# Two of the four additions of each post norm moved to GpSimd, and the output stored by quarters

## The chip, the cores and the metric

The kernel runs on one core of a Trainium2 chip. The metric is the device time of one execution in microseconds; the median of several executions stands for a kernel. All times below are in microseconds unless marked otherwise.

## The reference, cut to what matters

The program computes three layers on a sequence of 256 tokens with 2048 features, in fp32: a first hybrid layer with a feed-forward part, an attention layer (`ev`) and a pooling layer (`od`). The two last ones end alike. The result of their output product is normalised over the features, multiplied by a gate and added to the residual:

```python
def _rmsnorm(x, g):
    xf = x.astype(jnp.float32)
    y = xf * lax.rsqrt(jnp.mean(xf * xf, axis=-1, keepdims=True) + EPS)
    return (y * g.astype(jnp.float32)).astype(x.dtype)

# end of the attention layer, then of the pooling layer
x = x + gate * _rmsnorm(y @ w_out, post_g)
```

Between them stands the pooling layer's first step, `h = _rmsnorm(x, pre_g) * (1 + scale) + shift`, and a product of `h` with a weight matrix. After the pooling layer `x`, 256 x 2048, is the output.

## The kernel before

Activations lie with features on the 128 partitions and tokens along the free axis: the residual `res` and the outputs of a product, `pr`, are 16 tiles of 128x256. Weights stream from HBM in halves of 512 KB (`w_main`, issued by SyncE). ScalarE rounds each to `w_hi`, VectorE makes the rest `w_lo`, and TensorE multiplies in three passes (lines 565 to 567). A second stream, `w_side`, is issued by GpSimd (line 490) and summed by VectorE into the modulation vectors.

Each engine has one program, and its order is the order in which the Python writes it; semaphores alone tie the engines together. An engine that waits holds back everything written behind the wait.

In the product before a post norm, VectorE reads each output tile times the gate into `pr` (line 1577), ScalarE squares it (line 1076) and GpSimd adds the squares up (`add_square`, line 531). TensorE then sums over the partitions with a matrix of ones (line 592), and `mean_to_rstd` turns that into `rstd` (line 1470, a square root on ScalarE at line 1103, a reciprocal at line 1472).

`post_norm` (lines 1492 to 1505) follows on VectorE. The 16 tiles are taken as four groups of four, 128x1024 each. For every group there is a product, `sq2 = pr * rstd` (line 1499), and an addition, `res = res + sq2` (line 1504), interleaved as product 0, product 1, addition 0, product 2, addition 1, product 3, addition 2, addition 3. Each addition increments the semaphore `ev_res` or `final`. The trace calls `sq2` simply `sq`, as it leaves numbers out of names.

After `ev_post`, the middle gap: ScalarE squares the groups of `res` in the order 0 to 3 (`squares`, line 1098), TensorE adds them with the matrix of ones (`norm`, line 650; eight instructions in the trace for a group of four tiles), and the next norm's `rstd`, its scaling and the product `od_u` follow.

After `od_post`, the end: TensorE transposes the groups of `res` in the order 0 to 3 (line 644 through `turn`), ScalarE copies the half with the first 128 tokens to `o_tok` (line 1397), VectorE the half with the last 128 (line 2121). VectorE's copies are written behind all of its `post_norm`. SyncE stores `o_tok` in four DMAs of 512 KB (line 479): features 0 to 1023 of the first and of the last tokens, then 1024 to 2047 of both, each behind a wait for its copies.

Of the kernel before, what the change touches and what calls it, by code (L numbers as in the profile page):

```python
# [29 lines left out]
P = 128  # L30
# [158 lines left out]

SUMMED = ("ffn", "ev", "ev_post", "od_post")
NORMS = ("ffn", "ev", "od")
ROOTS = ("ffn", "ev", "ev_post", "od", "od_post")
# [49 lines left out]
def build(nc, x, ctx_in, w_main, w_side, cols_in, cons_in, gla_masks_in, counts_in, gate_w2_in, cmp_w2_in, out):  # L244
    stack = ExitStack()
    with stack:
# [182 lines left out]
        @block.sync  # L429
        def _(sp):  # L430
            sp.dma_start(cons[:, 0:2 * P], cons_in[:, 0:2 * P]).then_inc(S("ident_in"), 16)
            for q in range(4):
                part = slice(q * D // 4, (q + 1) * D // 4)
                sp.dma_start(x_tok[:, :, part], x.rearrange("(a p) d -> p a d", p=P)[:, :, part])\
                  .then_inc(S(f"x_in{q}"), 16)
                if q == 0:
                    sp.dma_start(cols[:, :], cols_in).then_inc(S("cols_in"), 16)
            for h in range(4):
                sp.dma_start(raw[:, h, :], w_main[stored_half(h // 2, h % 2)]).then_inc(raw_full[h], 16)
            sp.dma_start(cons[:, 2 * P:NCONS], cons_in[:, 2 * P:NCONS]).then_inc(S("small_in"), 16)  # L440
            sp.dma_start(table[:, 0:7 * P], gla_masks_in).then_inc(S("small_in"), 16)
            sp.dma_start(gate_w2[0:16, :], gate_w2_in).then_inc(S("small_in"), 16)
            sp.dma_start(cmp_w2[:, :, :], cmp_w2_in).then_inc(S("small_in"), 16)

            def load(i, h, at):

                sp.wait_ge(lo_ready, i * 4 + (h - 3))
                src = w_main[at] if isinstance(i, int) else w_main[bass.ds(i * 4 + at, 1)].rearrange("a p n -> (a p) n")
                sp.dma_start(raw[:, h % 4, :], src).then_inc(raw_full[h % 4], 16)

            def loads(stage):

                s0, s1 = max(FIRST[stage], 2), FIRST[stage] + COUNT[stage]
                stored = 2 * (STORED[stage] - FIRST[stage])

                def pair(i, s, count=2):
                    for h in range(2 * s, 2 * (s + count)):
                        load(i, h, h + stored)
                with sp.Fori(0, (s1 - s0) // 2) as i:
                    pair(i, s0)  # L460
                if (s1 - s0) % 2:
                    pair(0, s1 - 1, 1)

            for h in range(4, 2 * FIRST_LAYER):
                load(0, h, stored_half(h // 2, h % 2))
            for stage, count in STAGES:
                if FIRST[stage] < FIRST_LAYER:
                    continue
                loads(stage)
                if stage == "down0":  # L470

                    sp.wait_ge(dve_read, dve_reads("down0"))
                    sp.dma_start(ctx_tok[:, :, :], ctx_in.rearrange("(a p) d -> p a d", p=P)).then_inc(S("ctx_in"), 16)
                    sp.dma_start(table[:, :], counts_in).then_inc(S("counts_in"), 16)
            for part in range(2):
                cut = slice(part * D // 2, (part + 1) * D // 2)
                for tt in range(TT):
                    sp.wait_ge(S(f"o_tok{tt}"), 2 * part + 2)
                    sp.dma_start(out[tt * P:(tt + 1) * P, cut], o_tok[:, tt, cut]).then_inc(S("stored"), 16)
            sp.wait_ge(S("stored"), 16 * 2 * TT)  # L480


        @block.gpsimd
        def _(pool):
# [35 lines left out]
            def add_square(n, k):  # L520

                at0 = square_at(SUMMED[n])
                if k == 0:
# [7 lines left out]
                pool.tensor_tensor(sq_sum[:, :], sq_sum[:, :], sq_tile[:, k % 2, :], ALU.add)\  # L531
                    .then_inc(S("squares_added"), 1)

            def mods_and_squares(m0, n):

                for k in range(16):
                    add_square(n, k)
                    side_load(0, m0 + k + 2 * CMP_HALVES, (mods_added, m0 + k - 1))
# [8 lines left out]
                add_square(1, k)  # L547
            mod_loads(group_start("ev_kv") + 2, group_start("ev_out") + 2)
            mods_and_squares(group_start("ev_out") + 2, 2)
            mod_loads(group_start("od_z") + 2, 2 * MOD_TILES)  # L550
            for k in range(16):
                add_square(3, k)


        @block.tensor
        def _(pe):
# [87 lines left out]
                return pe.transpose(ps[0:ncols, bank, at_col:at_col + rows], src_ap, ident[base:base + rows, base:base + rows])  # L644

            def norm(name, bank=2):
                for q in range(4):
                    pe.wait_ge(S(f"{name}_sq"), q + 1)
                    for f in range(4 * q, 4 * q + 4):
                        mm = pe.matmul(ps[:, bank, 0:T], ones, sq[:, f, :], start=f == 0, stop=f == 15)  # L650
                mm.then_inc(S("sums_ready"), 1)
# [367 lines left out]
                    sum_mods("od_z")  # L1019
            pe.wait_ge(silu_ready, FFN_TILES + 33)  # L1020
            run("od_out", (b_hi, b_lo), split=[("gate_lo", FFN_TILES + 16)], summed="od_post")
            for g in range(4):
                pe.wait_ge(S("final"), g + 1)
                for tt in range(TT):
                    for f in range(4 * g, 4 * g + 4):
                        mm = turn(res[:, f, tt * P:(tt + 1) * P], 4 * tt + g, (f % 4) * P)
                    mm.then_inc(S("o_t"), 1)
# [26 lines left out]
        def _(act):  # L1054
# [38 lines left out]
                    square(0, COUNT[stage] - 1)  # L1093

            def squares(name, src, dst, wait):
                for q in range(4):
                    wait(q)
                    act.activation(dst[:, 4 * q:4 * q + 4, :], src[:, 4 * q:4 * q + 4, :], ACT.Square)\
                       .then_inc(S(f"{name}_sq"), 1)
# [263 lines left out]
            root("ev_post", rstd[:, :])  # L1363


            squares("od", res, sq, lambda q: act.wait_ge(S("ev_res"), q + 1))
            root("od", rstd[:, :])
            shift_hi("od", sq, a_hi, lambda f: mods[:, 48 + f, 0:1])
            def pool_chain():
# [22 lines left out]
                       .then_inc(S("od_hi"), 1)  # L1392
            ahead("od_out", squared="od_post")
            root("od_post", rstd[:, :])
            for g in range(4):
                act.wait_ge(S("o_t"), 2 * g + 1)
                act.activation(o_tok[:, 0, g * 512:(g + 1) * 512], ps[:, g, :], ACT.Copy).then_inc(S("o_tok0"), 1)


# [1 line left out]
        def _(dve):  # L1401
# [89 lines left out]
                                                       op0=ALU.add, op1=ALU.subtract)  # L1491
                    ins.then_inc(S("norm_lo"), 1)

            def post_norm(name, done):

                mean_to_rstd(name, ps[:, 2, 0:T], rstd[:, :], D)
                for q in range(5):
                    if q < 4:
                        dve.tensor_tensor(sq2[:, 4 * q:4 * q + 4, :], pr[:, 4 * q:4 * q + 4, :], cbc(rstd[:, :], 4), ALU.mult)\
                           .then_inc(S(f"{name}_y"), 1)  # L1500
                    if q > 0:
                        part = slice(4 * q - 4, 4 * q)
                        dve.wait_ge(S(f"{name}_y"), q)
                        dve.tensor_tensor(res[:, part, :], res[:, part, :], sq2[:, part, :], ALU.add)\
                           .then_inc(S(done), 1)

            link = S("dve_link")
            links = [0]
# [536 lines left out]

            reading("ev_z", z_read(0, 16, (a_hi, a_lo)), chain=chain)
            reading("ev_out", gated_read(ev_gate))
            post_norm("ev_post", "ev_res")
            dve.wait_ge(S("ev_res"), 4)


            dve.wait_ge(S("mods_read"), MOD_STAGES.index("ev_z") + 1)
# [62 lines left out]
            dve.wait_ge(S("mods_read"), len(MOD_STAGES))  # L2115
            then(dve.tensor_tensor(od_gate[:, :], mods[:, 80:96, 0], col("od_post", 0, 16), ALU.mult))
            reading("od_out", gated_read(od_gate))
            post_norm("od_post", "final")
            for g in range(4):
                dve.wait_ge(S("o_t"), 2 * g + 2)  # L2120
                dve.tensor_copy(o_tok[:, 1, g * 512:(g + 1) * 512], ps[:, 4 + g, :]).then_inc(S("o_tok1"), 1)


# [117 lines left out]
```

## Time and profile before

| | before |
|---|---|
| median of 3 executions | 2099.07 |
| lowest, highest | 2090.81, 2099.28 |
| the profiled execution | 2097.16 |
| its span | 2095.2 |
| TensorE busy | 2040.4 (97%) |
| VectorE busy | 1561.3 (75%) |
| ScalarE busy | 895.0 (43%) |
| GpSimd busy | 171.9 (8%) |
| TensorE's mean granted clock | 0.984 |

The span runs from the first to the last instruction of the profiled execution; the time of that execution is 1.96 longer. Busy times are sums over the span; they say little of the two gaps that the change touches, which last some ten microseconds each and are read from the timelines.

### The profile page before, as it was taken

Reading aid. Unit: us, or ns where it says so; the run is one execution under the profiler, and the core shown is the slowest. Engines: PE = TensorE matmul, PEld = TensorE weight load, DVE = VectorE, ACT = ScalarE, POOL = GpSimd, SP = SyncE. Lnnn points to the kernel's source line nnn. Section 1 sums busy time; section 2 is a strip of 40 time slices with the busy share of each in tenths; the row PEclk is TensorE's granted clock in tenths of the full one; section 3 lists DMA queues with packets and bytes.
Section 4 is the critical chain, followed back from the end, with each engine's and each line's share of the span. In section 5 each row is a group of like instructions: output and inputs, shape, how many; then the busy total and the mean of one; then the engine's idle time right before and its main releaser. Section 6 shows DMA issues by size and latency. Waiting matters only on the chain.

```text
span 2095.2 us, 41764 instructions
## 1 busy us (share of the span) xinstructions
PE 2040.4 (97%) x16266; PEld 1988.4 (95%) x16266; DVE 1561.3 (75%) x2056; ACT 895.0 (43%) x1178; POOL 171.9 (8%) x264
## 2 busy tenths in 40 slices
PE   7999999999999999999999998999999997999997
PEld 6999998899999999999999998998889996999996
DVE  6985576657777867787878888678887777677755
ACT  6553446554343334333333454235454444344442
POOL 0000000021000000000011111010000120000010
PEclk9999999999999999999999999999999998999998
DMA  6444453255666776666878864565556772558552
GB/s 229 161 162 136 167 184 119 101 178 205 230 228 224 261 277 222 228 224 236 272 259 295 299 224 172 172 247 197 199 171 224 262 274 105 192 204 277 195 187 98
DMA packets 119578, 434.46 MB, mean 207 GB/s; under 512 B 13216, under 2 KB 13600, under 8 KB 119216
## 3 DMA queue, kind: packets, MB, share of 16 engines
q1 hardware_dynamic: 90672, 328.11, 45.8%
q0 software_dynamic: 28800, 104.87, 14.2%
q8 instruction: 74, 1.21, 0.2%
q14 instruction: 32, 0.26, 0.0%
HBM read 430.83 MB, written 2.10 MB: 207 GB/s over the span
## 4 chain that ended last, share of the span: by engine, by line
PE 90%; DVE 7%; ACT 1%; issue 1%; DMA 1%; POOL 0%; SPq 0%; POOLq 0%; DVEq 0%; ACTq 0%
PE ps L565 27%; PE ps L567 26%; PE ps L566 26%; DVE w_lo L1407 2%; PE ps L644 1%; PE ps L968 1%; PE ps L639 1%; PE ps L978 1%; PE ps L683 1%; ACT w_hi L1062 0%; DVE pr L1563 0%; PE ps L674 0%; PE ps L919 0%; PE ps L650 0%; DVE rstd L1472 0%
## 5 line engine op out<-in xcount | busy, mean ns | idle before, releaser
L1062 ACT ACTIVATE w_hi<-raw 128x1024 fp32r<-128x1024 f32 x610 | 632.3, 1055 | 638.0 <-PE ps L567 625.5
L565 PE MATMUL ps<-a_hi,w_hi 128*128 128x256 f32 x3024 | 865.2, 286 | 6.3 <-DVE a_lo L1490 4.3
L566 PE MATMUL ps<-a_lo,w_hi 128*128 128x256 f32 x3024 | 858.3, 284 | 0.0
L567 PE MATMUL ps<-a_hi,w_lo 128*128 128x256 f32 x3024 | 858.1, 284 | 0.0
L1407 DVE TENSOR_TENSOR w_lo<-raw,w_hi 128x1024 fp32r<-128x1024 f32 x610 | 734.8, 1246 | 109.7 <-ACT w_hi L1062 108.6
L565 PEld LDWEIGHTS ps<-a_hi,w_hi 128*128 128x128 f32 x3024 | 583.2, 193 | 12.3 <-issue 7.5
L566 PEld LDWEIGHTS ps<-a_lo,w_hi 128*128 128x128 f32 x3024 | 583.4, 193 | 1.0 <-issue 1.0
L567 PEld LDWEIGHTS ps<-a_hi,w_lo 128*128 128x128 f32 x3024 | 583.0, 193 | 0.0
L565 PE MATMUL ps<-b_hi,w_hi 128*128 128x256 f32 x1920 | 553.6, 288 | 5.2 <-DVE b_lo L1490 4.6
L566 PE MATMUL ps<-b_lo,w_hi 128*128 128x256 f32 x1920 | 546.5, 285 | 0.0
L567 PE MATMUL ps<-b_hi,w_lo 128*128 128x256 f32 x1920 | 546.5, 285 | 0.0
L565 PEld LDWEIGHTS ps<-b_hi,w_hi 128*128 128x128 f32 x1920 | 371.7, 194 | 7.8 <-issue 7.2
L566 PEld LDWEIGHTS ps<-b_lo,w_hi 128*128 128x128 f32 x1920 | 371.9, 194 | 1.5 <-issue 1.4
L567 PEld LDWEIGHTS ps<-b_hi,w_lo 128*128 128x128 f32 x1920 | 371.8, 194 | 0.0
L1424 DVE SCALAR_TENSOR_TENSOR mod_sum<-side,csil,mod_sum 128x1024 f32<-128x1024 f32 x180 | 228.0, 1280 | 10.7 <-DMA side<-w_side 7.1
L490 POOL DMA_DIRECT2D side<-w_side x200 | 109.1, 546 | 1462.9 <-DVE mod_sum L1424 822.9
L1040 ACT ACTIVATE sg<-up_x 128x256 f32<-128x256 f32 x44 | 18.4, 417 | 232.5 <-DVE up_x L1934 232.5
L1424 DVE SCALAR_TENSOR_TENSOR mod_odd<-side,csil,mod_odd 128x1024 f32<-128x1024 f32 x60 | 74.2, 1278 | 0.6 <-DMA side<-w_side 0.6
L1934 DVE TENSOR_TENSOR up_x<-ps,rstd 128x256 f32<-128x256 f32 x88 | 37.0, 421 | 47.3 <-PE ps L567 47.2
L1582 DVE TENSOR_TENSOR pr<-ps,rstd 128x256 f32<-128x256 f32 x29 | 12.3, 423 | 69.7 <-PE ps L567 69.7
L531 POOL TENSOR_TENSOR sq_sum<-sq_sum,sq_tile 128x256 f32<-128x256 f32 x45 | 42.0, 933 | 192.8 <-ACT sq_tile L1076 192.8
L1841 DVE TENSOR_TENSOR res<-ps,res 128x256 f32 (+1 forms) x48 | 20.3, 423 | 33.4 <-PE ps L567 33.3
(308 smaller groups left out, 1291.2 us busy)
## 6 DMA issues: line engine op xcount, KB each, us to landing
raw<-w_main SPq DMA_DIRECT2D x610, 512.0 KB, 4.3
side<-w_side POOLq DMA_DIRECT2D x200, 512.0 KB, 4.5
x_tok<-x_in SPq DMA_DIRECT2D x4, 512.0 KB, 7.4
ctx_tok<-ctx_tok SPq DMA_DIRECT2D x1, 2048.0 KB, 11.4
y_out<-o_tok SPq DMA_DIRECT2D x4, 512.0 KB, 3.2
table<-counts_tab SPq DMA_DIRECT2D x1, 512.0 KB, 12.9
cons<-cons_in SPq DMA_DIRECT2D x1, 478.0 KB, 10.4
table<-masks_in SPq DMA_DIRECT2D x1, 448.0 KB, 10.3
```

Of the source, the lines that this page charges most:

```text
L490: pool.dma_start(side[:, n % 2, :], src).then_inc(side_full[n % 2], 16)
L531: pool.tensor_tensor(sq_sum[:, :], sq_sum[:, :], sq_tile[:, k % 2, :], ALU.add)\
L565: pe.matmul(out_ap, wh, act_hi[:, kt, :], start=first and n == 0, stop=False)
L566: pe.matmul(out_ap, wh, act_lo[:, kt, :], start=False, stop=False)
L567: mm = pe.matmul(out_ap, wl, act_hi[:, kt, :], start=False, stop=last and n == len(blocks) - 1)
L639: mm = pe.matmul(ps[:, MOD_BANK.get(stage, 7), vecs * t + c:vecs * t + c + 1], summed[c][:, t * P:(t + 1) * P], ones[:, 0:1], start=True, ...
L644: return pe.transpose(ps[0:ncols, bank, at_col:at_col + rows], src_ap, ident[base:base + rows, base:base + rows])
L683: mm = pe.matmul(ps[:, 7, 32 * kv:32 * kv + 2 * N_CMP], side[:, c % 2, b * P:(b + 1) * P], n_x[:, kv, j, :], start=j == 0, stop=j == CMP_W ...
L1062: act.activation(w_hi[:, slot, :], raw[:, slot, :], ACT.Copy).then_inc(hi_ready, 1)
L1407: dve.tensor_tensor(w_lo[:, slot, :], raw[:, slot, :], w_hi[:, slot, :].bitcast(F32), ALU.subtract)\
L1424: ins = dve.scalar_tensor_tensor(out=summed[c], in0=side[:, n % 2, :], scalar=value, in1=summed[c], op0=ALU.mult, op1=ALU.add)
L1934: dve.tensor_tensor(up_x[:, k % 2:k % 2 + 1, :], psum_tile(bank), rstd_row, ALU.mult)\
```

## The change

The constant `POST_ORDER = (0, 2, 1, 3)` is new. VectorE makes all four products, in the order 2, 0, 3, 1, and the additions of groups 0 and 1. GpSimd adds groups 2 and 3, each behind a wait for its product. ScalarE's squares, TensorE's sums, the transposes and the copies take the groups in the order 0, 2, 1, 3. The semaphores `post_added` and `post_pool` replace `ev_res` and `final`. The output goes out in eight DMAs of 256 KB, by groups of 512 features.

```diff
+POST_ORDER = (0, 2, 1, 3)
@@ sync
-            for part in range(2):
-                cut = slice(part * D // 2, (part + 1) * D // 2)
+            for n, g in enumerate(POST_ORDER):
+                part = slice(g * 512, (g + 1) * 512)
                 for tt in range(TT):
-                    sp.wait_ge(S(f"o_tok{tt}"), 2 * part + 2)
-                    sp.dma_start(out[tt * P:(tt + 1) * P, cut], o_tok[:, tt, cut]).then_inc(S("stored"), 16)
-            sp.wait_ge(S("stored"), 16 * 2 * TT)
+                    sp.wait_ge(S(f"o_tok{tt}"), n + 1)
+                    sp.dma_start(out[tt * P:(tt + 1) * P, part], o_tok[:, tt, part]).then_inc(S("stored"), 16)
+            sp.wait_ge(S("stored"), 16 * 4 * TT)
@@ gpsimd
+            def post_additions(name):
+
+                for q, made in ((2, 1), (3, 3)):
+                    part = slice(4 * q, 4 * q + 4)
+                    pool.wait_ge(S(f"{name}_y"), made)
+                    pool.tensor_tensor(res[:, part, :], res[:, part, :], sq2[:, part, :], ALU.add)\
+                        .then_inc(S("post_pool"), 1)
...
             mods_and_squares(group_start("ev_out") + 2, 2)
+            post_additions("ev_post")
             mod_loads(group_start("od_z") + 2, 2 * MOD_TILES)
             for k in range(16):
                 add_square(3, k)
+            post_additions("od_post")
@@ tensor
             def norm(name, bank=2):
-                for q in range(4):
-                    pe.wait_ge(S(f"{name}_sq"), q + 1)
+                for n, q in enumerate(POST_ORDER):
+                    pe.wait_ge(S(f"{name}_sq"), n + 1)
...
-            for g in range(4):
-                pe.wait_ge(S("final"), g + 1)
+            for g in POST_ORDER:
+                pe.wait_ge(S("post_added" if g < 2 else "post_pool"), g % 2 + 3)
@@ scalar
             def squares(name, src, dst, wait):
-                for q in range(4):
+                for q in POST_ORDER:
...
-            squares("od", res, sq, lambda q: act.wait_ge(S("ev_res"), q + 1))
+            squares("od", res, sq, lambda q: act.wait_ge(S("post_added" if q < 2 else "post_pool"), q % 2 + 1))
...
-            for g in range(4):
-                act.wait_ge(S("o_t"), 2 * g + 1)
+            for n, g in enumerate(POST_ORDER):
+                act.wait_ge(S("o_t"), 2 * n + 1)
@@ vector
-            def post_norm(name, done):
+            def post_norm(name):
 
                 mean_to_rstd(name, ps[:, 2, 0:T], rstd[:, :], D)
-                for q in range(5):
-                    if q < 4:
-                        dve.tensor_tensor(sq2[:, 4 * q:4 * q + 4, :], pr[:, 4 * q:4 * q + 4, :], cbc(rstd[:, :], 4), ALU.mult)\
-                           .then_inc(S(f"{name}_y"), 1)
-                    if q > 0:
-                        part = slice(4 * q - 4, 4 * q)
-                        dve.wait_ge(S(f"{name}_y"), q)
-                        dve.tensor_tensor(res[:, part, :], res[:, part, :], sq2[:, part, :], ALU.add)\
-                           .then_inc(S(done), 1)
+
+                def part(q):
+                    return slice(4 * q, 4 * q + 4)
+
+                def product(q):
+                    dve.tensor_tensor(sq2[:, part(q), :], pr[:, part(q), :], cbc(rstd[:, :], 4), ALU.mult)\
+                       .then_inc(S(f"{name}_y"), 1)
+
+                def addition(q, made):
+                    dve.wait_ge(S(f"{name}_y"), made)
+                    dve.tensor_tensor(res[:, part(q), :], res[:, part(q), :], sq2[:, part(q), :], ALU.add)\
+                       .then_inc(S("post_added"), 1)
+
+                product(2)
+                product(0)
+                addition(0, 2)
+                product(3)
+                product(1)
+                addition(1, 4)
...
-            post_norm("ev_post", "ev_res")
-            dve.wait_ge(S("ev_res"), 4)
+            post_norm("ev_post")
+            dve.wait_ge(S("post_added"), 2)
+            dve.wait_ge(S("post_pool"), 2)
...
-            post_norm("od_post", "final")
-            for g in range(4):
-                dve.wait_ge(S("o_t"), 2 * g + 2)
+            post_norm("od_post")
+            for n, g in enumerate(POST_ORDER):
+                dve.wait_ge(S("o_t"), 2 * n + 2)
```

## Rows read from the trace of the kernel before

**Rows 1.** The page, the chain that ended last: shares of the span by engine.
```profile
PE 90%; DVE 7%; ACT 1%; issue 1%; DMA 1%; POOL 0%; SPq 0%; POOLq 0%; DVEq 0%; ACTq 0%
```

**Rows 2.** The same chain, its end: start, duration, what.
```profile
2079.16 2.36 DVE sq L1499 x2
...
2086.06 2.27 DVE res L1504 x2
2088.33 1.80 DVE o_tok L2121 x3
```

**Rows 3.** Timeline of VectorE after `ev_out`: start, duration, instruction, idle time before.
```profile
1747.29 2.36 DVE L1499 TENSOR_TENSOR sq<-pr,rstd 128x1024 f32<-128x1024 f32 x2
1749.57 1.22 DVE L1504 TENSOR_TENSOR res<-res,sq 128x1024 f32<-128x1024 f32 x1
...
1754.11 2.35 DVE L1504 TENSOR_TENSOR res<-res,sq 128x1024 f32<-128x1024 f32 x2
```

**Rows 4.** Timeline of ScalarE after `ev_out`.
```profile
1750.82 1.06 ACT L1098 ACTIVATE sq<-res 128x1024 f32<-128x1024 f32 x1 [5.35 <-DVE res L1504]
```

**Rows 5.** Timeline of TensorE after `ev_out`.
```profile
1751.93 8.85 PE L650 MATMUL ps<-sq,cons 128*128 128x256 f32 x32 [7.37 <-ACT sq L1098]
```

**Rows 6.** Windows, line 650: length, TensorE busy, weight loads, granted clock, DMA share, GB/s.
```profile
1751.90:1755.30 3.40, 3.37 (x8) 2.74 (x9) 0.50 0.00 0
1755.40:1760.80 5.40, 5.38 (x25) 4.38 (x24) 1.00 0.01 3
```

**Rows 7.** Timeline of GpSimd, additions of 128x256 in three stretches.
```profile
1737.63 0.94 POOL L531 TENSOR_TENSOR sq_sum<-sq_sum,sq_tile 128x256 f32<-128x256 f32 x1 [4.29 <-ACT sq_tile L1076]
...
2035.02 0.95 POOL L531 TENSOR_TENSOR sq_sum<-sq_sum,sq_tile 128x256 f32<-128x256 f32 x1 [4.79 <-ACT sq_tile L1076]
...
2074.91 0.72 POOL L531 TENSOR_TENSOR sq_sum<-sq_sum,sq_tile 128x256 f32<-128x256 f32 x1 [5.02 <-ACT sq_tile L1076]
```

**Rows 8.** Timeline of GpSimd, additions of 128x512.
```profile
444.05 2.37 POOL L517 TENSOR_TENSOR f_sum<-f_sum,f_sq 128x512 f32<-128x512 f32 x1 [4.85 <-ACT f_sq L1267]
...
478.32 1.30 POOL L517 TENSOR_TENSOR f_sum<-f_sum,f_sq 128x512 f32<-128x512 f32 x1 [3.10 <-ACT f_sq L1267]
```

**Rows 9.** Groups of GpSimd by line, shapes apart: busy, mean ns, idle before.
```profile
L502 POOL MEMSET g_k<- 128x1024 f32 x1 | 1.0, 954 | 0.0
```

**Rows 10.** Timeline of VectorE beside the first of rows 8.
```profile
442.92 2.35 DVE L1407 TENSOR_TENSOR w_lo<-raw,w_hi 128x1024 fp32r<-128x1024 f32 x2
```

**Rows 11.** Timeline of VectorE beside the first two of rows 7.
```profile
1737.88 1.76 DVE L1407 TENSOR_TENSOR w_lo<-raw,w_hi 128x1024 fp32r<-128x1024 f32 x1
...
2034.16 2.89 DVE L1407 TENSOR_TENSOR w_lo<-raw,w_hi 128x1024 fp32r<-128x1024 f32 x2
```

**Rows 12.** Timeline of ScalarE, the last square of `od_out`.
```profile
2074.45 0.38 ACT L1076 ACTIVATE sq_tile<-ps 128x256 f32<-128x256 f32 x1 [5.37 <-DVE pr L1577]
```

**Rows 13.** Timeline of VectorE at the end.
```profile
2088.25 2.47 DVE L2121 COPY o_tok<-ps 128x512 f32<-128x512 f32 x4
```

**Rows 14.** Timeline of TensorE at the end.
```profile
2082.71 1.97 PE L644 MATMUL ps<-cons,res 128*128 128x128 f32 x8 [6.28 <-DVE res L1504]
...
2087.25 2.23 PE L644 MATMUL ps<-cons,res 128*128 128x128 f32 x16 [0.49 <-DVE res L1504]
```

**Rows 15.** Windows at the end: busy times by engine, granted clock, DMA share, GB/s.
```profile
2082.00:2087.00 5.00, 3.75 (x16) 3.11 (x16) 5.00 (x5) 1.20 (x2) 0.00 (x0) 0.56 0.00 0
2087.00:2090.00 3.00, 2.19 (x16) 1.72 (x16) 3.00 (x5) 1.19 (x2) 0.00 (x0) 1.00 0.43 175
...
2090.50:2091.50 1.00, 0.00 (x0) 0.00 (x0) 0.23 (x1) 0.00 (x0) 0.00 (x0) 1.00 1.00 401
```

**Rows 16.** Line 479, SyncE's issues of the stores: ns min/median/max, first and last start.
```profile
L479 SPq DMA_DIRECT2D y_out<-o_tok x4: 348/392/453, 2086.8 to 2090.8; - x4
DMA to landing us min/median/max: 2.6/3.2/4.1
```

## The prediction

> **What bounds the kernel now.** I read the page's chain of waits first: TensorE carries 90% of it and VectorE 7% [rows 1]. The kernel is a row of matrix stages that keep TensorE full, and everything this change edits lies in two of the gaps between them: after the product `ev_out` (post norm `ev_post`, then the next norm's squares and sums) and after `od_out` (post norm `od_post`, then transposes, copies and stores). Nothing in the matrix stages is touched, so the question is only how long these two gaps get.
>
> The chain's end shows the last gap: eight VectorE instructions from 2079.16 to 2088.33, then VectorE's copies, then the stores [rows 2]. VectorE is in sequence on it all the way. The earlier gap has the same eight from 1747.29 on; the first addition ends at 1749.57 + 1.22 = 1750.79 and the last at 1754.11 + 2.35 = 1756.46 [rows 3]. Here only the first addition sets the end: ScalarE squares its group at once, 1.06 [rows 4], TensorE starts its sums at 1751.93 and runs them for 8.85 without a gap [rows 5]. So the middle gap is bound by the first addition and then by TensorE, with eight instructions for each of the four groups. Eight of the 32 fall into the 3.40 with a granted clock of 0.50 (1.2 GHz), 25 (one of them reaches in from before) into the 5.40 with 1.00 (2.4 GHz) [rows 6]: a group takes 8 x 0.43 = 3.4 at the low level and 8 x 0.216 = 1.73 at the full one. The squares of the last two additions are ready before TensorE wants them.
>
> **What the change does, part by part.** VectorE issues six instead of eight: product 2, product 0, addition 0, product 3, product 1, addition 1. GpSimd does additions 2 and 3. VectorE's start-to-start distance is 1.14 (a pair of 2.36 less 1.22) [rows 3].
>
> *GpSimd's addition of 128x1024.* No row has it. Alone, 128x256 takes 0.72 [rows 7] and 128x512 takes 1.30 [rows 8], so 0.58 for each further 256 columns: 1.30 + 2 x 0.58 = 2.46, an estimate. Bounds: twice the 512 row, 2.60, and from below a GpSimd instruction of that width that only writes, 0.95 [rows 9]. I take 2.46, as the rows are of the same operation. The Trainium skill (GPSIMD Engine Reference, Performance versus the Vector engine) gives 4497 ns for an addition of 2048 elements, half of which is 2.25; by that every figure below with two GpSimd additions would be 0.4 lower.
>
> *Do the two engines run beside each other?* This decides the sign. The six VectorE instructions all have both inputs in SBUF, and so do GpSimd's. The trace has such pairs. At 444.05 a GpSimd addition takes 2.37 while VectorE makes `w_lo`; at 478.32, with VectorE nearly idle, the same takes 1.30 [rows 8]: 1.07 more, about one VectorE instruction, and that VectorE pair took its usual 2.35 [rows 10]. The other way round, VectorE's `w_lo` at 1737.88 took 1.76 where 1.22 is usual; GpSimd's addition ended at 1737.63 + 0.94 = 1738.57, and VectorE ended 1.07 after that [rows 7, 11]. At 2034.16 a back-to-back pair took 2.89 instead of 2.35, and GpSimd, which had asked at 2035.02 in the middle of the first, took 0.95 [rows 7, 11]: it got in at 2035.97 - 0.72 = 2035.25, before the second of the pair. So they exclude each other, and a waiting GpSimd is served at the next boundary between VectorE instructions. What no row has is a GpSimd instruction of four times that width holding VectorE. I take it that the whole 2.46 is held, since in both rows VectorE was kept until GpSimd's end and not for a share of it; the other bound is no hold at all. The Trainium skill (SBUF — State Buffer, practical consequences) says that a VectorE instruction with two SBUF inputs contends with a GpSimd instruction that reads SBUF, and that the one that starts first keeps the shared ports for the whole instruction. By that rule the whole 2.46 is held; by the rows alone only about 0.7 is proven.
>
> *The timetable,* from the start of the first product, with full exclusion. Product 2 ends at 1.22, product 0 at 2.36. GpSimd is woken at 1.30 (0.08 from ScalarE's end 2074.83 to GpSimd's 2074.91 [rows 7, 12]), waits for product 0 and gets in at 2.23 (0.13 before its recorded end, as at 2035.25). Addition 0 has to wait for product 0's end, so GpSimd is first: addition 2 runs to 4.69. Addition 0 ends 1.07 later, at 5.76, where before it ended at 3.50. Product 3 ends at 6.89 and product 1 at 8.03; addition 3 gets in at 7.90 and ends at 10.36; addition 1 ends at 11.43. Before, all was done at 9.17. The added waits themselves (a VectorE instruction on the one just before it, twice) cost at most 0.1 each and lie inside GpSimd's time here. Each addition that is moved takes 1.14 off VectorE and puts 2.46 between two VectorE instructions.
>
> *Middle gap.* Addition 0 ends at 1747.29 + 5.76 = 1753.05, its square at 1754.14, TensorE starts at 1754.25 instead of 1751.93. Group 0 at the low clock lasts to 1757.7, group 2 to 1759.4. Addition 1 ends at 1758.72, its square at 1759.8, and the square of group 3 at 1760.9. Group 1 runs from 1759.9 to 1761.6, group 3 to 1763.4. With the same tail of about 0.1 that is 1763.5, where it was 1751.93 + 8.85 = 1760.78: **+2.7**. All after it hangs on these sums (rstd, `a_hi`, `a_lo`, `od_u`) and moves with them. Behind GpSimd's new waits stand only the side loads of the next modulation groups, whose data VectorE adds from `od_u` on; hidden, and at 0.
>
> *End.* Addition 1 ends at 2079.16 + 11.43 = 2090.59 instead of 2088.33 for the last of before. VectorE's copies (2.47 for four, 0.60 apart [rows 13]) come behind it: groups 0 and 2 end at 2091.2 and 2091.8. Groups 1 and 3 need transposes: 16 take 2.23 at full clock, 8 take 1.97 at the low one [rows 14]; the clock was low at 2082 to 2087 and full after [rows 15]. The last copy ends between 2093.3 and 2094.9. The stores: eight of 256 KB instead of four of 512 KB, on SP in one queue. The first leaves early, the second has to wait for VectorE's first copy at 2091.2, and six more stand behind it, also ScalarE's, which were long ready. An issue takes 0.39 [rows 16]; seven of 0.42 apart put the last at 2093.8 or later. At 401 GB/s [rows 15] 256 KB take 0.65, and seven 4.6. Before, the last of the four was issued at 2090.8 and 4.1 is the longest time to landing [rows 16], so about 2094.9. Its 1.57 MB with the two ahead of it take 3.9 at that rate, so they began at 2090.6 at the latest, and I put the data 0.9 behind the first of their issues, an estimate (VectorE's second copy, for which it waits, ends 2089.6). Now: 2091.2 + 0.9 + 4.6 = 2096.7, landing noted 0.4 later, and the rest of the span 0.4: 2097.5 against 2095.2, **+2.3**. If quarters travelled worse than 512 KB pieces the term would be up to 1 higher; if they let the data start earlier, 0.5 lower.
>
> **Sum.** +2.7 + 2.3 = +5.0. The profiled execution took 2097.16 with a span of 2095.2, so 2102.2 on its own basis. The median of the three runs shown is 1.9 above it, 2099.07, which gives 2104.1. I name 2103.1, between the two. With 0.95 for GpSimd's addition the timetable would have addition 0 at 4.25 and addition 1 at 8.41: +0.8 and about -1.0, so -0.2 in all; with 2.60 it is +5.4.
>
> **Rivals.**
> - *The two engines run side by side after all* (the other side: not slower). Its place is both timetables, and the point from which it decides is a GpSimd addition that ends while VectorE's instructions keep 1.22. Addition 0 ends at 3.6, addition 2 at 3.8, addition 3 and addition 1 at 7.2 instead of 9.17. The middle gap gains nothing, since TensorE is its bound (+0.1). At the end copies finish at about 2089.0 and stores, still one after another, at 2093.2: -2.0. Together -1.9: 2097.2 from the median, 2095.3 from the profiled execution. For it: nothing but that no row has this width. Against it: [rows 7, 8, 11].
> - *VectorE wins the port at the boundary*, because addition 0 needs product 0's end and is quick to ask. Then addition 0 ends at 3.6, addition 2 at 5.9, addition 1 at 9.4 and addition 3 at 11.7. Middle +1.2, end +1.0: +2.2: 2101.3 from the median, 2099.4 from the profiled execution, 2100.3 between them. Against it: GpSimd was served within a back-to-back pair [rows 7, 11].
> - *TensorE's clock stays low in the middle gap,* since TensorE now idles 9.7 instead of 7.4 before the sums [rows 5], then has a short hole ahead of group 1. Groups at 3.4 each from 1754.25: 1768.0, so +7.3 there; with slower transposes (+1) and the rest, +10.6: 2108.7, on the same footing as the forecast. For it: the first 3.4 of before were at 1.2 GHz. Against it: the clock rose about 3.4 after TensorE began, with the same kind of work [rows 6].
>
> **Chances.** Full exclusion, GpSimd first: 0.64. Side by side 0.12, VectorE first 0.12, low clock 0.12. All lie within 0.5% (10.5) of 2099.07, which is about what a measurement of this kernel can tell from no change. The three runs shown spread from 2090.81 to 2099.28, more than any rival moves, so a median may come out low for that reason alone (2103.1 - 8 = 2095). The range: 2094.5 to 2108. Faster by over 0.5% needs under 2088.6: 0.02. Slower by over 0.5% needs over 2109.6, the low clock and some more: 0.05. Same 0.93.
>
> **What would show it.** GpSimd's first addition of each post norm is recorded with 3.3 to 3.5 (2.46 and a wait of 0.9), the second likewise; VectorE's additions with over 3 instead of 1.22. TensorE's sums of the middle gap start 2.3 later and have a hole before their third group. SP's last seven issues follow one another without gaps from the first VectorE copy. I am wrong if VectorE's additions stay at 1.22 while GpSimd is at work, if GpSimd's additions are recorded under 2, or if the time before the middle gap differs between the two traces by more than these gaps do.

## The result, and the profile after

| | before | after |
|---|---|---|
| median | 2097.24 (20 executions) | 2099.25 (20 executions) |
| lowest, highest | 2090.63, 2100.57 | 2096.79, 2106.4 |
| span of the profiled execution | 2095.2 | 2096.7 |
| reciprocal to reciprocal in the middle gap | 16.30 | 19.06 |
| last reciprocal to the end of the span | 17.77 | 20.64 |

The ratio of after to before is 1.0022, with a 95% interval from 1.0011 to 1.0032: the change costs some 4.6 (2.3 to 6.7). The means say the same (2095.86 and 2100.47), while the medians are only 2.0 apart. The prediction named +5.0 and 2103.1, within 0.5%; the median came out 3.9 lower. Each of the five `rstd` ends in one reciprocal on VectorE, so the last three serve as marks: the middle gap is read from the third to the fourth, the end from the fifth. (The tails here and below are counted to some 0.05 before the end of the span, in all kernels alike, so their differences hold.) The middle gap grew by 2.76 and the end by 2.87, 5.6 together. The span grew by 1.5 only, because the stages ahead of both gaps, where the two kernels are the same, were shorter by 4.0 in this execution; the last section comes back to that.

Timeline of GpSimd after the change, both gaps (start, duration, instruction, idle time before it):

```profile
1744.56 3.24 POOL L540 TENSOR_TENSOR res<-res,sq 128x1024 f32<-128x1024 f32 x1 [4.27 <-DVE sq L1513]
1750.10 3.26 POOL L540 TENSOR_TENSOR res<-res,sq 128x1024 f32<-128x1024 f32 x1 [2.29 <-DVE sq L1513]
...
2079.13 3.25 POOL L540 TENSOR_TENSOR res<-res,sq 128x1024 f32<-128x1024 f32 x1 [4.79 <-DVE sq L1513]
2084.68 3.26 POOL L540 TENSOR_TENSOR res<-res,sq 128x1024 f32<-128x1024 f32 x1 [2.29 <-DVE sq L1513]
```

Timeline of VectorE in the middle gap, the answer to [rows 3]:

```profile
1741.45 1.75 DVE L1483 RECIPROCAL rstd<-rstd 128x256 f32<-128x256 f32 x1 [0.48 <-ACT rstd L1114]
1743.24 2.36 DVE L1513 TENSOR_TENSOR sq<-pr,rstd 128x1024 f32<-128x1024 f32 x2
1745.64 3.25 DVE L1518 TENSOR_TENSOR res<-res,sq 128x1024 f32<-128x1024 f32 x1
1748.81 2.35 DVE L1513 TENSOR_TENSOR sq<-pr,rstd 128x1024 f32<-128x1024 f32 x2
1751.18 3.25 DVE L1518 TENSOR_TENSOR res<-res,sq 128x1024 f32<-128x1024 f32 x1
```

VectorE's additions are recorded with 3.25 instead of 1.22, GpSimd's with 3.25 as well. Count from the first product at 1743.24: addition 2 ends at 4.56, addition 0 at 5.65, addition 3 at 10.12, addition 1 at 11.19. The timetable had 4.69, 5.76, 10.36 and 11.43. Each pair runs one after the other. If addition 0 works for the last 1.07 of its record, as the prediction assumed, it gets its operands at 4.58, which is 2.2 after product 0 ended at 2.36.

TensorE in the middle gap, timeline and then windows of line 661 (length, busy, weight loads, granted clock, DMA share, GB/s), the answers to [rows 5, 6]:

```profile
1750.03 9.47 PE L661 MATMUL ps<-sq,cons 128*128 128x256 f32 x32 [9.52 <-ACT sq L1109]
```

```profile
1750.20:1755.00 4.80, 4.80 (x12) 3.87 (x13) 0.53 0.00 0
1755.10:1759.80 4.70, 4.39 (x21) 3.53 (x19) 1.00 0.02 3
```

TensorE starts 1743.24 + 6.79, which is 2.15 later than before, and then runs 9.47 instead of 8.85. There is no hole ahead of its third group; the clock came back to 2.4 GHz some 4.7 after it began, not 3.4 as in [rows 6].

The end, from the chain of waits (start, duration, what), the answer to [rows 2], and SyncE's issues, the answer to [rows 16]:

```profile
2077.83 2.37 DVE sq L1513 x2
2080.20 0.02 issue
2080.22 3.24 DVE res L1518
2083.47 2.28 DVE sq L1513 x2
2085.75 0.02 issue
2085.77 3.27 DVE res L1518
2089.04 0.04 issue
2089.08 3.69 PE ps L655 x16
2092.77 0.02 issue
2092.80 0.69 DVE o_tok L2143
```

```profile
L480 SPq DMA_DIRECT2D y_out<-o_tok x8: 332/349/455, 2085.3 to 2093.5; - x8
DMA to landing us min/median/max: 2.5/3.0/3.4
```

The last addition ends at 2089.02, the last 16 transposes run at the low clock, and the last copy ends at 2093.49, 15.66 after the first product (11.6 before). From there the span lasts 3.2, where it lasted 4.5. VectorE's first two copies, from its timeline:

```profile
2088.95 1.27 DVE L2143 COPY o_tok<-ps 128x512 f32<-128x512 f32 x2
```

A single copy takes 0.69, so the first ends at 2089.64: 11.8 after the first product, and 7.1 before the end of the span. Before the change these were 9.8 and 6.3. The last issue, at 2093.5, starts as the last copy ends, so the issues do not follow one another without gaps.

### The profile page after: what moved, and what is told of

Read it like the earlier page. It is cut to its first block, busy times and chain, and to the rows that moved or that the text cites. A ratio compares the mean times of both kernels' runs of the same rounds, so it can differ in the third digit from the quotient of the medians.

```text
span 2096.7 us, 41768 instructions
## 1 busy us (share of the span) xinstructions
PE 2038.5 (97%) x16266; PEld 1986.6 (95%) x16266; DVE 1564.8 (75%) x2052; ACT 894.9 (43%) x1178; POOL 185.3 (9%) x268
## 4 chain that ended last, share of the span: by engine, by line
PE 90%; DVE 7%; ACT 1%; issue 1%; DMA 0%; POOL 0%; SPq 0%; ACTq 0%; DVEq 0%; POOLq 0%
PE ps L576 27%; PE ps L577 27%; PE ps L578 27%; DVE w_lo L1418 2%; PE ps L655 2%; PE ps L979 1%; PE ps L989 1%; PE ps L650 1%; PE ps L694 1%; ACT w_hi L1073 0%; DVE res L1518 0%; DVE pr L1584 0%; PE ps L661 0%; PE ps L685 0%; PE ps L930 0%
```

## The experiments

Marks used below: *middle* is from the third to the fourth reciprocal, *tail* from the fifth to the end of the span, *copy* from the fifth reciprocal to the end of VectorE's last copy. Before: 16.30, 17.77, 13.4. After: 19.06, 20.64, 17.45. In all kernels the stretch from the fourth to the fifth reciprocal is 315.5 to 315.8.

**VectorE's operands in PSUM.**

```diff
-                mean_to_rstd(name, ps[:, 2, 0:T], rstd[:, :], D)
+                rp = ps[:, 3, 0:T]
+                held = ps[:, 6:8, :].rearrange("p b (a t) -> p (b a) t", a=2)
+                mean_to_rstd(name, ps[:, 2, 0:T], rstd[:, :], D, to=rp)
...
-                    dve.tensor_tensor(sq2[:, part(q), :], pr[:, part(q), :], cbc(rstd[:, :], 4), ALU.mult)\
+                    dve.tensor_tensor(sq2[:, part(q), :] if q > 1 else held, pr[:, part(q), :], cbc(rp, 4), ALU.mult)\
...
-                    dve.tensor_tensor(res[:, part(q), :], res[:, part(q), :], sq2[:, part(q), :], ALU.add)\
+                    dve.tensor_tensor(res[:, part(q), :], res[:, part(q), :], held, ALU.add)\
```

> The changed kernel, but rstd and the products of groups 0 and 1 lie in PSUM, so that no VectorE instruction of the post norms has two inputs in SBUF; the arithmetic is the same. Theory A (the engines exclude each other through the second SBUF read of VectorE): GpSimd's additions are recorded with 2.35 and no wait, VectorE's additions with about 1.2 instead of 3.25; the last addition ends 7.2 after the first product instead of 11.2; first product to first product of the two post norms 331.9 as before the change (334.6 after), end gap 14.3 to 15.3 (16.0 before, 18.9 after); time 4 to 5.5 under the changed kernel, 0 to 2 under the one before. Theory B (any work of both engines on SBUF excludes): GpSimd's additions stay at 3.25, VectorE's too, time as changed.

Ratio to before 0.9993 (0.9979 to 1.0007). Timelines of GpSimd and of VectorE in its middle gap:

```profile
1751.98 2.34 POOL L540 TENSOR_TENSOR res<-res,sq 128x1024 f32<-128x1024 f32 x1 [4.28 <-DVE sq L1515]
1755.49 2.36 POOL L540 TENSOR_TENSOR res<-res,sq 128x1024 f32<-128x1024 f32 x1 [1.17 <-DVE sq L1515]
```

```profile
1750.67 1.22 DVE L1515 TENSOR_TENSOR sq<-pr,ps 128x1024 f32<-128x1024 f32 x1
1751.81 1.22 DVE L1515 TENSOR_TENSOR ps<-pr,ps 128x1024 f32<-128x1024 f32 x1
1753.06 1.22 DVE L1520 TENSOR_TENSOR res<-res,ps 128x1024 f32<-128x1024 f32 x1
1754.20 1.21 DVE L1515 TENSOR_TENSOR sq<-pr,ps 128x1024 f32<-128x1024 f32 x1
1755.33 1.22 DVE L1515 TENSOR_TENSOR ps<-pr,ps 128x1024 f32<-128x1024 f32 x1
1756.59 1.22 DVE L1520 TENSOR_TENSOR res<-res,ps 128x1024 f32<-128x1024 f32 x1
```

Theory A holds for the two engines. GpSimd works from 1751.98 to 1754.32 beside three VectorE instructions, and neither is slowed. All additions are done 7.2 after the first product. This kernel differs from the changed one in where VectorE's operands lie, in one wait of VectorE on its own addition, and in the PSUM banks of the transposes; the 2.03 of each VectorE addition and the 0.9 of each GpSimd addition were the second SBUF input. The middle is 17.15, though, not the 16.3 that came with the expected 331.9 from first product to first product (332.7 measured). TensorE began its sums 4.75 after the first product, nearly as early as the 4.64 of before the change, but took 9.57 for them instead of 8.85:

```profile
1755.42 9.57 PE L661 MATMUL ps<-sq,cons 128*128 128x256 f32 x32 [7.50 <-ACT sq L1109]
```

The granted clock of this stretch was 0.50 up to 3.6 after its start and 0.78 in the next 3.0, so it stayed low for longer. The tail is 16.6, 1.2 under the 17.77 of before.

**GpSimd only writes.**

```diff
-                    pool.tensor_tensor(res[:, part, :], res[:, part, :], sq2[:, part, :], ALU.add)\
+                    pool.memset(res[:, part, :], 0.0)\
```

> The changed kernel, but GpSimd only fills groups 2 and 3 of the residual with zeros instead of adding (the additions of these groups are left out). Theory A (GpSimd's reads are what VectorE's second input excludes): GpSimd's fill is recorded with 0.95, VectorE's additions with 1.22, also where they overlap. Theory B (any SBUF use excludes): the fill waits for the product in progress and is recorded with about 1.8, VectorE's addition with 1.22 plus what is left of the fill, 1.8 or so.

```profile
1742.62 0.94 POOL L540 MEMSET res<- 128x1024 f32 x1 [4.25 <-DVE sq L1513]
```

```profile
1741.33 2.36 DVE L1513 TENSOR_TENSOR sq<-pr,rstd 128x1024 f32<-128x1024 f32 x2
1743.72 1.23 DVE L1518 TENSOR_TENSOR res<-res,sq 128x1024 f32<-128x1024 f32 x1
```

The fill lies inside VectorE's second product, whose two inputs lie in SBUF, and takes the same 0.95 as alone [rows 9]. So the clash is of reads. The Trainium skill (SBUF — State Buffer, practical consequences) says both things: a VectorE instruction with at most one SBUF input, outside its 2-port modes, does not contend with GpSimd, and one with two contends with a GpSimd instruction that reads SBUF, not with one that only writes it. These two kernels agree: 2.34 and 1.22 side by side in the first, 0.94 for the fill in the second.

**One addition moved instead of two.**

```diff
-                for q, made in ((2, 1), (3, 3)):
+                for q, made in ((2, 1),):
...
+                addition(3, 3)
                 addition(1, 4)
```

> The changed kernel with only the addition of group 2 on GpSimd; VectorE adds group 3 between product 1 and addition 1. Theory A (each moved addition takes 1.14 off VectorE and puts about 2.3 of GpSimd between two VectorE instructions): one addition of VectorE recorded with 3.25, the others 1.22, the last ends 10.1 to 10.4 after the first product (9.17 with none moved, 11.2 with two). Theory B (a cost of the change that does not grow with the number, such as the added waits): 11 or more.

```profile
1747.16 2.36 DVE L1513 TENSOR_TENSOR sq<-pr,rstd 128x1024 f32<-128x1024 f32 x2
1749.56 3.25 DVE L1520 TENSOR_TENSOR res<-res,sq 128x1024 f32<-128x1024 f32 x1
...
1755.00 2.35 DVE L1520 TENSOR_TENSOR res<-res,sq 128x1024 f32<-128x1024 f32 x2
```

Theory A holds. The last addition ends 10.19 after the first product (1755.00 + 2.35 less 1747.16): 9.17, 10.19, 11.19 for none, one and two. Each moved addition costs VectorE's row 1.0. The tail follows, with 19.8 between the 17.77 and 20.64 of none and two.

**The stores.**

```diff
-            for n, g in enumerate(POST_ORDER):
-                part = slice(g * 512, (g + 1) * 512)
+            for part in range(2):
+                cut = slice(part * D // 2, (part + 1) * D // 2)
                 for tt in range(TT):
-                    sp.wait_ge(S(f"o_tok{tt}"), n + 1)
+                    sp.wait_ge(S(f"o_tok{tt}"), part + 3)
```

> The changed kernel with the stores in four DMAs of 512 KB as before the change, the order of groups kept. Theory A (the quarters give time back at the end): 2 MB leave only after the third copy, end gap 18.9 + 1.2 = 20.1, the middle as changed; time about 1.2 over the changed kernel. Theory B (eight issues in SyncE's queue cost what they give): end gap 18.5 to 19.1.

Ratio to before 1.0019 (1.0009 to 1.003), tail 21.71, copy 17.44: in the changed kernel the quarters save 1.1 of tail behind the same last copy. In the profile this is Theory A (20.0 from the first product to the end, 20.1 expected); the times can't tell the two kernels apart.

The other way round, quarters in the kernel before:

```diff
-            for part in range(2):
-                cut = slice(part * D // 2, (part + 1) * D // 2)
+            for g in range(4):
+                cut = slice(g * 512, (g + 1) * 512)
                 for tt in range(TT):
-                    sp.wait_ge(S(f"o_tok{tt}"), 2 * part + 2)
+                    sp.wait_ge(S(f"o_tok{tt}"), g + 1)
```

> The kernel before with the stores in eight DMAs of 256 KB, by groups 0 to 3, nothing else. Theory A: the last copy and the queue of seven issues behind VectorE's first copy bind, end gap 15.7 to 16.1 (16.04 before), no change of time. Theory B (smaller last stores shorten the tail as such): end gap 15.0 or less.

And its stores of 512 KB cut by partitions:

```diff
-                    sp.dma_start(out[tt * P:(tt + 1) * P, cut], o_tok[:, tt, cut]).then_inc(S("stored"), 16)
+                    for r in range(2):
+                        sp.dma_start(out[tt * P + 64 * r:tt * P + 64 * (r + 1), cut],
+                                     o_tok[64 * r:64 * (r + 1), tt, cut]).then_inc(S("stored"), 16)
```

> The kernel before with each store of 512 KB cut into two DMAs by partitions (64 rows each of 4 KB), so eight issues, but rows as long as before. Theory A (rows of 2 KB made the stores by quarters slow): tail from the last reciprocal 17.5 to 18.2, near the 17.77 of before and under the 19.8 of the kernel with quarters. Theory B (eight issues one behind the other made it slow): 19 or more.

With quarters the ratio is 1.0002 (0.9989 to 1.0014), the tail 19.80 and the copy 13.35 as before, so 6.4 behind the last copy instead of 4.4. With cuts by partitions the tail is 20.01 and the copy 14.25 (the last transposes fell into the low clock), 5.8 behind it. Windows of the kernel with quarters (last three columns: granted clock, DMA share, GB/s):

```profile
2086.00:2087.00 1.00, 0.00 (x0) 0.00 (x0) 0.00 (x0) 0.00 (x0) 0.00 (x0) 1.00 1.10 217
...
2089.00:2090.00 1.00, 0.00 (x0) 0.00 (x0) 0.00 (x0) 0.00 (x0) 0.00 (x0) 0.50 1.15 242
```

The DMA engines are busy throughout and yet move 217 and 242 GB/s in these two windows, where 401 were reached [rows 15]. Neither expectation foresaw this for the quarters: both had 16.1 or less from the first product to the end, and 18.1 were measured. For the cuts by partitions Theory B holds. They have rows of 4 KB and were slow too, so short rows can't be the whole cause. But each such store also covers 64 partitions instead of 128, so this kernel does not clear row length altogether. What the two slow kernels share is eight small stores packed close together; what in them costs the time stays open.

**TensorE kept at work in the gaps.**

```diff
+            for _ in range(16):
+                pe.matmul(ps[:, 0, 0:T], ones, cons[:, 0:T], start=True, stop=True)
             norm("od")
...
             run("od_out", (b_hi, b_lo), split=[("gate_lo", FFN_TILES + 16)], summed="od_post")
+            for _ in range(13):
+                pe.matmul(ps[:, 0, 0:T], ones, cons[:, 0:T], start=True, stop=True)
```

> The kernel before, with products of constants into an unused PSUM bank on TensorE in the two gaps: 16 before the sums after ev_post, 13 before the transposes after od_post. Theory A (the low clock is a cost of the middle gap and not of the end): TensorE's 32 sum instructions take 6.9 to 7.2 instead of 8.85, reciprocal to reciprocal in the middle gap 14.4 to 14.8 instead of 16.3; the end as before, since VectorE's additions and copies bind it; time 1.5 to 2 less. Theory B (the clock level does not follow what TensorE does here): 8.85 and 16.3 again, no change.

Ratio 0.9987 (0.997 to 1.0004); middle 15.71, tail 17.77. TensorE's sums in the kernel before with constants:

```profile
1751.56 1.99 PE L650 MATMUL ps<-sq,cons 128*128 128x256 f32 x8 [0.47 <-ACT sq L1102]
1753.83 1.99 PE L650 MATMUL ps<-sq,cons 128*128 128x256 f32 x8 [0.28 <-ACT sq L1102]
1756.10 3.72 PE L650 MATMUL ps<-sq,cons 128*128 128x256 f32 x16 [0.28 <-ACT sq L1102]
```

A group takes 1.99 at the full clock, but the sums now wait for the squares of the next addition, 2.27 apart. I had expected 14.4 to 14.8 and forgot this second limit: the clock's share is 0.6, not 1.7. The same in the changed kernel, with 20 and 18 in place of 16 and 13:

> The changed kernel with such products in the gaps (20 and 18). Theory A: the sums now wait for the squares of groups 1 and 3, so that the hole before the third group appears; reciprocal to reciprocal in the middle gap 18.3 to 18.6 instead of 19.06, that is 2.0 to 2.3 over the 16.3 of before without the clock; the last transposes take about 1.9 instead of 3.68 if the clock lasts over the hole of 1.9 before them, and the tail from the last reciprocal is 19 to 20 instead of 20.6. Theory B: 19.06 and 20.6 again.

```profile
1748.69 3.72 PE L661 MATMUL ps<-sq,cons 128*128 128x256 f32 x16 [0.89 <-ACT sq L1113]
1754.25 3.72 PE L661 MATMUL ps<-sq,cons 128*128 128x256 f32 x16 [1.84 <-ACT sq L1113]
```

Ratio 1.0015 (1.0003 to 1.0028); middle 18.89, tail 20.68. The hole of 1.84 ahead of the third group, absent from the changed kernel, is there at once. With the clock out of the way in both, the moved additions cost the middle 18.89 - 15.71 = 3.2. The expectation was missed in both gaps (18.3 to 18.6 for the middle, 19 to 20 for the tail): at the end the clock fell again in the hole of 3.6 before the last transposes, which took 3.67. One more kernel fills that too:

```diff
             for g in POST_ORDER:
+                if g == 1:
+                    for _ in range(8):
+                        pe.matmul(ps[:, 1, 0:T], ones, cons[:, 0:T], start=True, stop=True)
```

> The changed kernel with products of constants on TensorE in both gaps (20 and 18) and 8 more between the transposes of the second and of the third group. Theory A (the low clock of the last 16 transposes is a term of the end): they take 1.97 instead of 3.68, the last copy ends 1.6 to 1.8 earlier (15.7 after the last reciprocal instead of 17.45); the tail 19.3 to 20.0 instead of 20.64, less than the copy gains, since the eight stores come closer together. Theory B (the stores bind whatever the copies do): 20.6 again.

```profile
2085.93 1.95 DVE L2150 COPY o_tok<-ps 128x512 f32<-128x512 f32 x3
2088.07 0.69 DVE L2150 COPY o_tok<-ps 128x512 f32<-128x512 f32 x1 [0.18 <-PE ps L655]
```

The last 16 transposes take 1.97 and the copy is 15.75, 1.7 earlier; the tail is 20.67. Theory B: nothing comes out of it, the stores bind. SyncE's last issue now starts at 2089.8, 1.0 after the last copy. The low clock of the last transposes, plain to see in the chain of the changed kernel, costs nothing there.

The other kernels bear this out. Six kernels store by quarters in the order 0, 2, 1, 3: the changed one, the one with operands in PSUM, the one with fills, the one with one addition moved, and the changed one with constants, in its two versions. From the end of VectorE's first copy to the end of the span they all take 7.1 to 7.2, while from the last copy they take anything from 3.2 to 4.9. In the kernel before with quarters, where the copies come closest together, the first figure is 8.3.

**The versions put together.** To the kernel with operands in PSUM comes another choice of groups, so that the stores can go by halves again:

```diff
-POST_ORDER = (0, 2, 1, 3)
+POST_ORDER = (0, 1, 2, 3)
...
-                for q, made in ((2, 1), (3, 3)):
+                for q, made in ((1, 1), (3, 3)):
...
-                product(2)
+                product(1)
                 product(0)
                 addition(0, 2)
                 product(3)
-                product(1)
-                addition(1, 4)
+                product(2)
+                addition(2, 4)
```

> The kernel with rstd and the products of VectorE's groups in PSUM, GpSimd adding groups 1 and 3, the groups in the order 0, 1, 2, 3, stores in four DMAs of 512 KB as before the change, and TensorE kept busy in both gaps (16 and 13). Theory A (contention, the low clock and the small stores were the three costs): no wait between GpSimd and VectorE; reciprocal to reciprocal in the middle gap 14.4 to 15; tail from the last reciprocal 15.5 to 16.2 against 17.77; time 3 to 4 under the kernel before. Theory B (the gain in VectorE's instructions goes on to some other engine at the end): tail 17 or more, time not over 2 under before.

> The kernel with rstd and products in PSUM, GpSimd adding groups 1 and 3, stores by halves, without the products of constants. Theory A (two costs, contention and stores, are gone, the clock's is left): middle gap 16.2 to 17.2 from reciprocal to reciprocal as in the kernel before; tail 16.3 to 17.2 against 17.77 to before; time 0.5 to 1.5 under before. Theory B (most of the gain of the version with constants came from the clock): time within 0.5 of before.

> The same with 11 products of constants in each gap instead of 16 and 13. With 16 they held the sums up by 0.9 (TensorE started 5.7 after the first product instead of 4.75). Theory A: sums start 4.75 after the first product at the full clock; middle gap 14.4 to 15.0, tail 16.2 to 16.6; time 3.5 to 5 under before. Theory B (11 are too few, the clock falls before the sums): 15.5 or more in the middle, time 2 to 3.5 under before.

| kernel | middle | tail | ratio to before |
|---|---|---|---|
| PSUM operands, halves, no constants | 17.17 | 16.44 | 0.9993 (0.9978 to 1.0008) |
| the same, 16 and 13 constants | 15.58 | 16.42 | 0.9979 (0.9963 to 0.9994) |
| the same, 11 and 11 constants | 14.83 | 16.43 | 0.9985 (0.9969 to 1.0) |

The second is faster than the kernel before by 0.2%, and its interval leaves 1 out. The third has the shorter gaps in its profile, but its time can't be told from the second's. By the ratios the two with constants are 4.4 and 3.1 under before, each with an interval of some 3 either way, where 3 to 4 and 3.5 to 5 were named: the times confirm the sign for the second and the size for neither. By the gaps, the second should gain 2.1 and the third 2.8. In the profile of the second both gaps missed what was expected (14.4 to 15 and 15.5 to 16.2), the middle because its constants held the sums up, 5.7 after the first product; with 11 constants the middle came out as expected. The tail gained 1.3 against before, with the copies 11.7 after the reciprocal instead of 13.4.

## Why the prediction was right, and where by luck

- *GpSimd's addition.* 2.46 by extrapolation; 2.35 measured. The 2.25 estimated from the Trainium skill's figure (GPSIMD Engine Reference, Performance versus the Vector engine) was as near from the other side. With the bound of 2.60 the prediction's own timetable gives about +5.6 in all, not the +5.4 that it names.
- *Exclusion.* Right, by the whole length of GpSimd's instruction, and GpSimd first at the boundary. Of the rivals, "side by side" is false as the kernel stood and true once VectorE's operands are in PSUM; there all additions were done at 7.2, as it had them, but the end gained 1.2 and not the 2.0 that it was priced at, and the middle lost 0.9 to the clock. "VectorE first" is false: additions 0 and 1 ended after 2 and 3, all four times.
- *Middle gap, +2.7 named, +2.76 measured,* but not by the step that I gave. I had TensorE at the full clock 3.4 after its start, then a hole ahead of group 1. The clock stayed low for 4.7, the hole was filled, and TensorE was the bound. Two chains end within 0.2 of each other: the kernel with constants shows the other one, 18.89. The rival of the low clock had its place right and was priced as if the low level lasted to the end of the sums.
- *The same code gives other middles.* The kernel before and its two versions with other stores, identical up to there, have 16.30, 16.10 and 17.08, by the clock alone (8.85 against 9.63 of sums in the last). The changed kernel and its version with halves have 19.06 and 18.87. So the term lies between 1.8 and 3.0, depending on which profiles are paired, and that +2.7 met +2.76 so closely is luck.
- *End, +2.3 named, +2.87 measured.* The last addition came 11.19 after the first product for 11.43, the last copy 15.66 after it, within the 14.1 to 15.7 that the prediction's 2093.3 to 2094.9 stand for. The step that is off is the store term: seven quarters at 401 GB/s. I had VectorE's first copy 2.3 later than before and nothing more behind it (6.3 from there to the end, as before). It came 2.0 later, and 7.1 followed, so the stores cost another 0.8. Quarters are slower than 401 GB/s when they stand close together, which I had allowed for with "up to 1 higher". That the stores behind VectorE's first copy bind, and not the last copy, is shown by the kernel in which the last copy came 1.7 earlier for nothing. That the last seven issues follow one another without gaps was wrong: the eighth waited for the last copy.
- *The time.* The named 2103.1 rests on a median of 2099.07 from three executions; over 20 it is 2097.24. With +5.0 on that it would be 2102.2, and 2099.25 was measured. The gaps grew by 5.6, the means by 4.6 and the medians by 2.0, so the time alone would not tell the forecast from its rival of +2.2; the rows do.

## What to carry to other kernels

Before moving elementwise work from VectorE to GpSimd, look in the profile for a pair of them that already overlap: if a 1.2 becomes 1.8 there, the move adds GpSimd's whole duration to VectorE's row, and what counts is the difference of the two engines' durations (here 2.35 less 1.14, or 1.2, of which 1.0 was measured). Putting one operand of each VectorE instruction into PSUM takes the clash away and is a small edit. And ask what the shortened row was hiding: here the middle gap was bound by TensorE's sums, so even a GpSimd that held nobody up gave nothing there until TensorE's clock was kept up (17.17 without constants, 14.83 with 11).

## What else the runs showed

The time of one execution spreads over 10, more than any kernel here gained or lost. In the profiled executions almost all of it lies between the first and the second reciprocal, in the feed-forward stages that no kernel touches: 790.8 before, 787.7 after, 783.1 with quarters. The clock does it. Four windows of 8.00 in the kernel before, then the same four in the kernel with quarters (busy of TensorE and number, weight loads, the other engines, granted clock, DMA share, GB/s):

```profile
669.00:677.00 8.00, 8.00 (x44) 8.00 (x44) 3.98 (x5) 0.01 (x1) 0.54 (x2) 0.57 0.74 270
768.00:776.00 8.00, 8.00 (x44) 8.00 (x44) 3.77 (x5) 1.44 (x3) 0.53 (x1) 0.57 0.69 241
959.00:967.00 8.00, 8.00 (x44) 8.00 (x44) 3.71 (x5) 0.60 (x1) 0.53 (x1) 0.57 0.79 278
1058.00:1066.00 8.00, 8.00 (x56) 8.00 (x56) 3.53 (x4) 1.86 (x2) 0.53 (x1) 0.79 0.72 250
```

```profile
669.00:677.00 8.00, 8.00 (x72) 8.00 (x71) 6.06 (x8) 2.06 (x2) 1.05 (x2) 1.00 0.89 305
768.00:776.00 8.00, 8.00 (x57) 8.00 (x57) 2.97 (x5) 1.18 (x2) 0.53 (x1) 0.79 0.66 207
959.00:967.00 8.00, 8.00 (x61) 8.00 (x60) 3.30 (x5) 2.12 (x2) 0.53 (x1) 0.86 0.63 215
1058.00:1066.00 8.00, 8.00 (x69) 8.00 (x68) 4.70 (x7) 2.12 (x2) 0.53 (x1) 1.00 0.50 156
```

At 0.57 TensorE gets through 44 products in 8.00, at 1.00 through 69 or 72, and it counts as busy in both. Which of these four places falls to 1.2 GHz, and for how long, differs from execution to execution of unchanged code; what decides it was not tried. For a change worth a few microseconds, distances inside the profile, from mark to mark, say more than the total.
